# Raw x transposed ahead of its norm at four places, and the first weight blocks in pieces

## The reference

```
_rmsnorm(x, g) = x * rsqrt(mean(x*x) + 1e-6) * g
x = x + 0.5 * _rmsnorm(_swiglu(_rmsnorm(x, ffn1_pre_g), w_gu, w_down), ffn1_post_g)
h = _rmsnorm(x, mix_pre_g)      # attention, state space, gates -> mixed
x = x + _rmsnorm(mixed @ w_mix_out, mix_post_g)
hq = _rmsnorm(x, xa_pre_g)      # 4 heads over mem, softmax -> xo
x = x + _rmsnorm(xo @ w_o, xa_post_g)
x = x + 0.5 * _rmsnorm(_swiglu(_rmsnorm(x, ffn2_pre_g), ...), ffn2_post_g)
h = rms_norm(x, g_norm)         # second block: c_q, c_kv, k_rope, z, hy, gates
_swiglu(h, w_gu, w_down): g, u = split(h @ w_gu); (silu(g) * u) @ w_down
```

## Time and profile before

| | |
|---|---|
| median of 3 runs | 1174.49 us (1174.33 to 1174.80) |
| the profiled execution's own time | 1174.42 us |
| its span | 1172.6 us |
| PE, PEld busy | 1150.1 us (98%), 1071.1 us (91%) |
| DVE, ACT busy | 757.4 us (65%), 582.2 us (50%) |
| mean granted TensorE clock | 0.994 |
| DMA queue of the weights | 45.1% of 16 engines' span |

### The profile page before, as it was taken

One profiled execution on the slowest core, in us unless ns is written; L12 is line 12 of the kernel. 1 busy time (PEld: TensorE's weight loads), 2 busy tenths in 40 slices (PEclk: granted clock), 3 DMA queues, 4 the chain that ended last, 5 costly groups with the idle time before them and its releaser, 6 DMA issues.

```text
span 1172.6 us, 20957 instructions
## 1 busy us (share of the span) xinstructions
PE 1150.1 (98%) x8558; PEld 1071.1 (91%) x8558; DVE 757.4 (65%) x1038; ACT 582.2 (50%) x828; POOL 0.2 (0%) x4
## 2 busy tenths in 40 slices
PE   8999999999999999999999999999999999999998
PEld 6999998999999999999996996999999599988898
DVE  6644446768898967677767646444555646984654
ACT  5434444567753335787445444444433447554351
POOL 0000000000000000000000000000000000000000
PEclk9999999999999999999999999999999999999999
DMA  8655555454453355453555234455555436443241
GB/s 313 224 190 183 195 188 186 164 196 149 175 169 118 109 165 177 144 179 113 212 165 195 93 109 162 144 184 187 194 186 179 143 108 218 144 144 108 72 144 37
DMA packets 28527, 189.61 MB, mean 162 GB/s; under 512 B 3400, under 2 KB 4713, under 8 KB 6378
## 3 DMA queue, kind: packets, MB, share of 16 engines
q1 hardware_dynamic: 25984, 181.41, 45.1%
q10 hardware_dynamic: 2474, 7.20, 1.8%
HBM read 187.55 MB, written 1.05 MB: 161 GB/s over the span
## 4 chain that ended last, share of the span: by engine, by line
PE 86%; DVE 8%; ACT 3%; issue 2%; DMA 1%; ACTq 0%; SPq 0%; DVEq 0%
PE bank L449 25%; PE bank L450 25%; PE bank L451 25%; PE bank L514 3%; DVE sb_w_lo L1775 2%; ACT sb_w_hi L1149 1%; DVE sb_ssd_conv L1945 1%; PE bank L681 1%; PE bank L1018 1%; PE bank L1006 1%; DMA sb_w_raw<-in_w 1%; PE bank L1040 1%; PE bank L1063 1%; PE bank L904 0%; PE bank L883 0%
## 5 line engine op out<-in xcount | busy, mean ns | idle before, releaser
L1775 DVE TENSOR_TENSOR sb_w_lo<-sb_w_raw,sb_w_hi 128x2048 fp32r<-128x2048 f32 x171 | 391.2, 2290 | 198.8 <-ACT sb_w_hi L1149 198.4
L449 PE MATMUL bank<-sb_hT_hi,sb_w_hi 128*128 128x256 f32 x1576 | 449.4, 285 | 0.4 <-DVE sb_hT_lo L1824 0.4
L450 PE MATMUL bank<-sb_hT_lo,sb_w_hi 128*128 128x256 f32 x1576 | 443.4, 281 | 0.0
L451 PE MATMUL bank<-sb_hT_hi,sb_w_lo 128*128 128x256 f32 x1576 | 443.2, 281 | 0.0
L1149 ACT ACTIVATE sb_w_hi<-sb_w_raw 128x2048 fp32r<-128x2048 f32 x171 | 326.8, 1912 | 108.1 <-PE bank L451 106.4
L449 PEld LDWEIGHTS bank<-sb_hT_hi,sb_w_hi 128*128 128x128 f32 x1576 | 297.1, 189 | 3.9 <-issue 2.7
L450 PEld LDWEIGHTS bank<-sb_hT_lo,sb_w_hi 128*128 128x128 f32 x1576 | 297.1, 188 | 2.4 <-issue 1.2
L451 PEld LDWEIGHTS bank<-sb_hT_hi,sb_w_lo 128*128 128x128 f32 x1576 | 296.9, 188 | 0.1
L449 PE MATMUL bank<-sb_w_hi,sb_hT_hi 128*128 128x256 f32 (+1 forms) x304 | 87.3, 287 | 2.1 <-DVE sb_w_lo L1775 1.1
L1197 ACT ACTIVATE sb_ffn_gate<-bank 128x256 f32<-128x256 f32 x44 | 16.9, 384 | 143.1 <-PE bank L451 143.1
L450 PE MATMUL bank<-sb_w_lo,sb_hT_hi 128*128 128x256 f32 (+1 forms) x304 | 85.0, 280 | 0.0
(11 more groups left out here) (388 smaller groups left out, 1673.0 us busy)
## 6 DMA issues: line engine op xcount, KB each, us to landing
sb_w_raw<-in_w SPq DMA_DIRECT2D x171, 1024.0 KB, 5.0
sb_x<-in_x SPq DMA_DIRECT2D x1, 1024.0 KB, 5.2
sb_mem_xn<-in_mem ACTq DMA_DIRECT2D x1, 1024.0 KB, 7.7
sb_post_g<-in_ffn_post_g ACTq DMA_DIRECT2D x2, 512.0 KB, 4.3
sb_dft_f<-in_c_dft ACTq DMA_DIRECT2D x1, 1024.0 KB, 6.6
out<-sb_x SPq DMA_DIRECT2D x4, 256.0 KB, 2.3
sb_post_g<-in_mix_post_g ACTq DMA_DIRECT2D x1, 512.0 KB, 5.5
sb_w_f<-in_w_f ACTq DMA_DIRECT2D x1, 512.0 KB, 5.1
```

The costliest lines, as they stand in the source:

```text
L449: pe.matmul(o, a_hi, b_hi, start=first, stop=False)
L450: pe.matmul(o, a_hi, b_lo, start=False, stop=False)
L451: return pe.matmul(o, a_lo, b_hi, start=False, stop=last)
L1775: tt(w_lo[b % STAGES][:], w_raw[b % RING][:], f32(w_hi[b % STAGES][:]), ALU.subtract).then_inc(w_lo_in, 1)
```

## The change

At four norms (the first FFN, xa, the second FFN, the second block) `raw_turn` transposes x itself, 128 tokens at a time as they are written, and `norm_high` and `norm_low` apply the gain and split it. The root is taken behind that and applied to the products. In the FFNs, `root_turn` transposes the root over 128 columns, ACT copies it to `rb`, and DVE multiplies the gate half with it ahead of silu; the up half stays unscaled, and the post-norm's eps is scaled instead (`post_eps`). In xa the root goes into softmax's scale (`xa_r`). In the second block cq, ckv and the rope part are made from the raw x and scaled per token on ACT; the z, hy and gate blocks use a normalized x as before, transposed by a further `norm_turn(6, ...)`.

`residual` writes x in three pieces, `last_block` gives the two token halves of the last output block a bank each, `stay_warm` goes from the mix stage, taps and spectra are placed before and after the transposes, and the filter's decay moves from xa into the xo stage. Block 0 of the weights is loaded, rounded and subtracted in 4 pieces, block 1 in 2, x in 2.

The diff, cut to its core:

```diff
-X_READY = [2, 4, 6, 8]
-POST_SSQ = [4, 8, 12, 16]
+X_READY = [3, 6, 9, 12]
+POST_SSQ = [4, 9, 14, 18]
+PARTS = {0: 4, 1: 2}
...
+            def last_block(key, b, a_hi, a_lo):
+                hi, lo = weights(b, KD, 256)
+                for t in range(TOK):
+                    o = claim(f"{key}.{t}", 7 if t else b % 3, b if t else None)
...
+            def raw_turn(n, landed, at=(3, 4, 5, 6)):
+                o = [claim(f"norm{n}.{kp}", at[kp]) for kp in range(KD // 2)]
+                for t in range(TOK):
+                    for k in range(KD):
+                        if k % 4 == 0:
+                            landed(t, k // 4)
+                        c = k % 2 * SEQ + t * P
+                        mm = turn(o[k // 2][:, c:c + P], x[:, t, k * P:(k + 1) * P])
+                        if t and k % 2:
+                            ends(mm, f"norm{n}.{k // 2}")
+            def root_turn(n):
+                pe.wait_ge(S("root"), n)
+                o = claim(f"rb{n}", 7)
+                for t in range(TOK):
+                    mm = turn(o[:, t * P:(t + 1) * P], xr[:, t:t + 1].to_broadcast([P, P]))
+                ends(mm, f"rb{n}")
...
                 for j in range(3):
                     up_block(j)
+                    if j == 0:
+                        root_turn(n)
...
-            for i in range(2, 4):
-                token_block(f"mix{i}", FIRST["mix_out"] + i, 256, mixed_hi, mixed_lo)
-            for i in range(8):
-                filter_taps(i)
-            stay_warm(hid[:, 3, 0:P], w_f3[:, 0:512], 4)
-            norm_turn(3, xa_xn)
+            token_block("mix2", FIRST["mix_out"] + 2, 256, mixed_hi, mixed_lo)
+            last_block("mix3", FIRST["mix_out"] + 3, mixed_hi, mixed_lo)
+            for i in range(6):
+                filter_taps(i, 3 + i % 4)
+            raw_turn(3, x_added(1), (5, 6, 3, 4))
+            for i in (6, 7):
+                filter_taps(i, 7 if i == 6 else (FIRST["xa_q"] + 1) % 3)
...
-            for i in range(3):
-                filter_spectrum(i, (3, 4, 5)[i])
-            norm_turn(4, ffn[2]["xn"])
+            for i in range(2):
+                filter_spectrum(i, 3 + i)
+            raw_turn(4, x_added(2), (5, 6, 3, 4))
+            filter_spectrum(2, (FIRST["ffn2"] + 1) % 3)
             ffn_part(2, 4)
-            for i in range(4):
-                filter_spectrum(4 + i, (0, 1, 2, 7)[i])
-            norm_turn(5, sec_xn)
-            token_block("cq0", FIRST["cq"], 256, hT_hi, hT_lo, ready=norm_done(5))
+            for i in range(2):
+                filter_spectrum(4 + i, i)
+            raw_turn(5, x_added(3))
+            for i in range(2, 4):
+                filter_spectrum(4 + i, 2 if i == 2 else 7)
+            token_block("cq0", FIRST["cq"], 256, sec_hi, sec_lo, ready=norm_done(5))
             token_block("ckv", ...)
+            norm_turn(6, sec_xn, 3)
             token_block("cq1", ...)
...
+            norm_high(0, "ffn1_pre_g", hT_hi, lambda kp: round_part(0, kp))
...
                 def hidden_tile(j, between, turn=0):
+                    o = full(dve, f"up{n}.{j}", turn)
+                    tt(f["gate"][:, j % 2, :], o[:, 0:SEQ], f["rb"][:], ALU.mult).then_inc(S("ffn_pre"), 1)
                     dve.wait_ge(S("ffn_gate"), done + j + 1 + 2 * turn)
...
-                for t in range(TOK):
-                    stt(x[:, t, :], y[:, t, :], rstd[:, 2 + t:3 + t], x[:, t, :], ALU.mult, ALU.add)
+                for t, c in ((0, slice(0, D)), (1, slice(0, D // 2)), (1, slice(D // 2, D))):
+                    stt(x[:, t, c], y[:, t, c], rstd[:, 2 + t:3 + t], x[:, t, c], ALU.mult, ALU.add)
...
+            def xo_between(i):
+                if i < 2:
+                    filter_decay(i)
+            out_part("xa_o", "xo", 2, xo_between)
```

More of the change, by code:

```diff
@@ L538, in norm_done, with part_done, landed @@
                 return ready
+            def part_done(b, ready):
+                parts = PARTS[b]
+                before = sum(PARTS[i] - 1 for i in range(b))
+                def landed(k):
+                    if k % (KD // parts) == 0:
+                        part = k // (KD // parts)
+                        if part < parts - 1:
+                            pe.wait_ge(S("part_lo"), before + part + 1)
+                        else:
+                            pe.wait_ge(w_lo_in, b + 1)
+                    if ready:
+                        ready(k)
+                return landed
             def ffn_part(n, norm):
@@ L567, in down_block @@
                                          c == 0 and k == 0, c == PAIRS - 1 and k == 1)
+                            if c == PAIRS - 1 and k == 1 and i < 3:
+                                ends(mm, f"down{n}.{i}")
                     mm.then_inc(block_done, 1)
@@ L1149, in round_block, with round_part @@
                 act.activation(w_hi[b % STAGES][:], w_raw[b % RING][:], ACT.Copy).then_inc(w_hi_in, 1)
+            def round_part(b, part):
+                n = BLOCK // PARTS[b]
+                c = slice(part * n, (part + 1) * n)
+                last = part == PARTS[b] - 1
+                act.wait_ge(w_landed[b] if last else S(f"part_landed{b}.{part}"), 16)
+                act.activation(w_hi[b][:, c], w_raw[b][:, c], ACT.Copy).then_inc(w_hi_in if last else S("part_hi"), 1)
+                rounded[0] = b + 1
             def round_to(n):
@@ L1206, in high @@
                     act.activation(f["hi"][:, j % 2, :], f["act"][:, j % 2, :], ACT.Copy).then_inc(S("ffn_hi"), 1)
+                o = full(act, f"rb{n}")
+                copy(f"rb{n}", f["rb"][:], o[:, 0:SEQ])
                 gate(0)
@@ L1256, in out_part @@
             def out_part(stage, key, i_post, between=None):
-                for i in range(4):
+                for i in range(3):
                     o = full(act, f"{key}{i}")
@@ L1268, in out_part @@
                         between(i)
+                for t in range(TOK):
+                    o = full(act, f"{key}3.{t}")
+                    act.wait_ge(S("post_ssq"), POST_SSQ[i_post - 1] + 3 + t)
+                    act.activation(post_tmp[:, t * 256:(t + 1) * 256], o[:, 0:256], ACT.Square,
+                                   accum_out=post_ssq[:, t, 3:4]).then_inc(S("post_ssq"), 1)
+                after(FIRST[stage] + 3)
             act.dma_start(ident, a["c_square"][:, 0:P]).then_inc(S("ident_in"), 16)
             act.dma_start(cols[:], a["cols"]).then_inc(S("cols_in"), 16)
-            act.wait_ge(S("x_in"), 16)
+            act.wait_ge(S("x_in0"), 16)
             norm_squares(x, ffn[1]["xn"])
-            round_to(1)
             act.wait_ge(S("cols_in"), 16)
-            norm_high(0, "ffn1_pre_g", hT_hi)
+            norm_high(0, "ffn1_pre_g", hT_hi, lambda kp: round_part(0, kp))
+            for part in range(PARTS[1]):
+                round_part(1, part)
             round_to(STAGES)
@@ L1536, in _ @@
             norm_squares(x, xa_xn)
-            for i in range(5, 8):
+            taps(5)
+            norm_high(3, "xa_pre_g", hT_hi)
+            for i in range(6, 8):
                 taps(i)
-            norm_high(3, "xa_pre_g", hT_hi)
             def xa_exps(h):
@@ L1775, in low_block, with low_part @@
                 tt(w_lo[b % STAGES][:], w_raw[b % RING][:], f32(w_hi[b % STAGES][:]), ALU.subtract).then_inc(w_lo_in, 1)
+            def low_part(b, part):
+                n = BLOCK // PARTS[b]
+                c = slice(part * n, (part + 1) * n)
+                last = part == PARTS[b] - 1
+                if last:
+                    dve.wait_ge(w_hi_in, b + 1)
+                else:
+                    dve.wait_ge(S("part_hi"), sum(PARTS[i] - 1 for i in range(b)) + part + 1)
+                tt(w_lo[b][:, c], w_raw[b][:, c], f32(w_hi[b][:, c]), ALU.subtract).then_inc(w_lo_in if last else S("part_lo"), 1)
+                lowered[0] = b + 1
             def low_to(n):
@@ L2509, in _ @@
         def _(sp):
-            sp.dma_start(x[:], a["x"].rearrange("(t p) d -> p t d", p=P)).then_inc(S("x_in"), 16)
+            for t in range(TOK):
+                sp.dma_start(x[:, t, :], a["x"][t * P:(t + 1) * P, :]).then_inc(S(f"x_in{t}"), 16)
             for b in range(RING):
-                sp.dma_start(w_raw[b][:], a["w"][b]).then_inc(w_landed[b], 16)
+                parts = PARTS[b] if b in PARTS else 1
+                for part in range(parts):
+                    c = slice(part * (BLOCK // parts), (part + 1) * (BLOCK // parts))
+                    sp.dma_start(w_raw[b][:, c], a["w"][b][:, c])\
+                        .then_inc(w_landed[b] if part == parts - 1 else S(f"part_landed{b}.{part}"), 16)
+            sp.wait_ge(S("part_lo"), sum(n - 1 for n in PARTS.values()))
             for i in range(2):
```

200 lines of the change are left out of this document (128 added, 72 removed).

## The result

| | before | after |
|---|---|---|
| median (lowest to highest) | 1174.8 us (1173.98 to 1174.88) | 1166.17 us (1162.11 to 1169.81) |
| profiled execution, its span | 1174.42, 1172.6 | 1168.75, 1167.0 |
| ratio to before | | 0.9928, 95% interval 0.9908 to 0.9948 |

8.6 us less, against a forecast of 3.4 less (1171.1; range 1168.0 to 1173.8). Both want an explanation. One execution of before in a later comparison took 1888.59 us at a mean granted clock of 0.555; no ratio here uses it.

The account below looks back on a forecast made before the run. PE, busy 98% of the span, bounds the kernel; its gaps total some 22 us. Terms 0 + 0.4 + 0.2 - 3.4 - 0.4 - 0.2 = -3.4 gave 1171.1 us, range 1168.0 to 1173.8.

Parts of the forecast that it names:

- these places: PE's largest gaps, at pre-norms: 4.22 us before xa_xn's transposes, 2.84 at the second FFN, 1.04 at the second block.
- mix to xa: Gap before the cross-attention's transposes stays about 4.1 us, clock down; xa_q starts earlier: -3.4, or -5.1 with the clock up.
- A slow stretch that reaches further into the taps: At mix to xa: low clock lasting past the transposes costs up to 1.7 us more, leaving -1.7 instead of -3.4.
- xo to the second FFN: PE waits 2.5 us before the second FFN's transposes: -0.4 with the clock down, -2.0 with it up.
- rival 1: Clock stays up in the xo gap (2.5 us) while mix falls: -1.6 more, 1169.5 us; chance 0.18.
- bank rule: raw_turn claims all four banks before its first transpose, so PE waits for ACT's copy: gaps 4.1 us (mix), 2.5 (xo).
- The first FFN's end: One more DVE pass makes ffn_lo late for PE's second half of the last block: +0.4 us.
- The second FFN: Turning the root there adds 0.2 us on PE; the longer end of its tile chain is covered by a spectrum.
- Second block: Moved spectra remove PE's wait, -1.9; 16 more transposes for the z blocks cost +1.75: net -0.2 us.
- Start: First FFN's up1 begins at 20.3 us against 20.28 before, chain starting when cols lands: 0, up to 1.2 either way.
- rival 4: Extra pass delays low halves in the FFN loops, half a microsecond in each of 18 turns: slower, 1180 us; chance 0.04.
- rival 2: Bank claims don't bind as ACT copies in time; mix gains 7.0, xo 4.5: 1163.4 us; chance 0.06.

Follow-up runs that it names:

- after_same_place: The kernel after with its three small tensors put into ssq's room, so hT_hi and all behind it lie as in before: 1172.74 us, ratio 0.9978.
- after_same_place_warm: The kernel after with the places of before, plus five and three 512-column constant products in PE's waits at cross-attention and second FFN: 1167.96 us, ratio 0.9941.
- before_pad96: The kernel before with one unused tensor of 96 bytes a partition ahead of hT_hi, nothing else: 1169.33 us, ratio 0.9955.
- after_bank7_xa: The kernel after with bank 7 instead of 4 for the fourth pair of raw transposes, at the cross-attention only: 1161.26 us, ratio 0.9885.

## Why the prediction was wrong, step by step

The table gives each stretch of the profiled executions in us, from the first product of one block to that of another; changes are against before. "Same place" is after_same_place, "filled" is after_same_place_warm.

| stretch | before | after | same place | filled |
|---|---|---|---|---|
| span start to first down block | 31.64 | -0.25 | -0.82 | +0.08 |
| to the first block of kv | 171.93 | +0.08 | +0.57 | +0.58 |
| to the first output block of mix | 405.01 | -2.03 | +0.07 | +0.22 |
| to the second query block | 54.38 | +1.00 | +1.09 | -4.47 |
| to the first block of xo | 28.69 | +0.32 | +0.35 | +0.36 |
| to the second FFN's first down block | 53.89 | -2.06 | -1.67 | -1.66 |
| to its last down block | 166.95 | -0.51 | 0.00 | 0.00 |
| to the z block ahead of c_q's products | 58.42 | -0.54 | -0.57 | -0.57 |
| to the end of the span | 201.7 | -1.7 | -0.5 | -0.5 |

**What failed.** The prediction said: "the change can win only at these places and at the start". Padding alone, without any of the change, wins 5.2 us (before_pad96), and the change without its shift of addresses 1.8 by the medians (after_same_place). The two add up to 7.0, of 8.6 measured; the rest is within the spread. The columns "after" and "same place" show where: 2.1 us in the mixer's input stages, 0.5 in each of the two FFNs, 1.2 at the end. The term that is missing is the place of the operands. The prediction doesn't mention the three small tensors, and so puts what they shift at nothing, without a reason; the profiled executions have it at 4.2 us (-5.7 in after, -1.5 in same place).

**mix to xa: the place and the wait right, the clock not.** Transposes waited for ACT's copy of the sixth taps, 4.18 us against 4.1 forecast, and with the places of before they start at 641.41, forecast 641.3. So this place was forecast as it came, up to the end of the gap. The step that failed is "A slow stretch that reaches further into the taps costs up to 1.7 more, -1.7": the slow stretch ran 13.65 us, so two taps' products took 3.78 us instead of 2.0 (1.8 more) and the first query block ran at 0.142 us a product instead of 0.119 (2.2 more). Instead of -3.4 this execution has +1.1, outside both bounds; with the clock held the same stretch has -4.5, near the -5.1 that the prediction gave for that case. So the term is worth from +1.1 to -4.5 by what the clock does. The twelve executions of same place spread by 5.5 us, and with both waits filled 1.0 is left, which ties the spread to these waits.

**xo to the second FFN: rival 1 in this execution.** The gap was 2.69 us (forecast 2.5), the bank rule was its cause, and the clock stayed up: -1.7 in same place, forecast -2.0 for that case. The Trainium skill (TensorE: Matmul & The Clock Gate, "Why this matters for your kernels") warns only of longer gaps; here after agrees with it at 2.69 us, but after_bank7_xa (2.70 us) and before (2.84 us) do not.

**The small terms.** The first FFN's end has the cost of the forecast, +0.57 in same place against +0.4, but at another place. The prediction had PE wait for ffn_lo. It is the transposes of the memory, ahead of the last down block, that wait longer for DVE's product with the gate; in before and in after:

```profile
196.75 1.09 PE L514 MATMUL bank<-sb_square,sb_mem_xn 128*128 128x128 f32 x8 [0.15 <-DVE sb_ffn_act L1841]
```

```profile
196.49 1.09 PE L535 MATMUL bank<-sb_square,sb_mem_xn 128*128 128x128 f32 x8 [0.64 <-DVE sb_ffn_act L1980]
```

From the end of ffn_lo to the product behind it there is 0.05 us as before (200.44 to 200.49). The second FFN: 0.2 forecast for the root's transposes; they lie ahead of its first down block, within -1.7. Second block: -0.57 against -0.2, and cq0 starts without a wait, with 16 transposes more. Start: up1 at 20.00, forecast 20.3; its root turn was at 19.81. But the start isn't one number: up1 stands 11.8 us behind the first transpose of x in each of the three kernels, and this transpose starts at 8.23 in after, 7.62 in same place and 8.52 in filled. So the chain began with the transposes and not with cols, as the prediction allowed, and the term came out between -0.8 and +0.1 where I took 0. The FFN loops are not delayed (0.00), so rival 4 falls, and rival 2 falls with both waits. I did not foresee +0.35 in the cross-attention, where PE waits 0.8 us for ACT's `xa_PT` instead of 0.4, nor -0.5 in the last stretch, where it waits 0.8 us for a w_lo instead of 1.1.

**Luck.** Without the shift of addresses the change brings 1.8 us by the medians and 1.5 in the profiled execution, half of the 3.4. Even that nearness is in part luck: the place that should have given nearly all of it, -3.4, has +1.1 there, and the start, xo, the second block and the end make up for it with -0.8, -1.7, -0.6 and -0.5.

**Still open.** Why d sets the spacing, what makes one block slower than another at the same d, and what chooses between the two rates at 64 and 192, no run tells. Nor do they tell why a gap of 2.7 us lowers the clock in one execution and not in another, or why the slow stretch is once 6.8 us and once 13.65.

## What to carry to other kernels

When the times move in stages that a change doesn't touch, compare the spacing of long runs of equal products first, and test it with an unused tensor as padding before explaining anything else: here that alone moved the kernel from 5 us faster to 9 slower. A helper that claims all its buffers at its start waits for the latest of them; give the last one a buffer that has long been read. And a wait of PE near 3 us or longer is worth filling with idle products even where it can't be shortened: the slow clock behind the gap of 2.70 us made the transposes take 3.32 us instead of 1.91, and filling the gap of 4.18 us took 5.6 us off its stretch (+1.1 to -4.5).
